# Two-layer diffusion-transformer block: two feed-forward weight chunks loaded into other buffers, and ScalarE's order at the turn from mixer to feed-forward

## The chip, the cores and the metric

The kernel runs on one core of one Trainium2 chip. Its time is the device time of one execution in microseconds (us). TensorE multiplies matrices, VectorE and ScalarE work element by element, GpSimd takes a few side jobs, and SyncE issues all DMA transfers. Engines run side by side, each in its own fixed order, and meet only at semaphores.

## What is computed

Two layers over 512 tokens of width 1024 with a context of 256 tokens. Cut to what matters here, one layer is

```python
x = x + g1x * mixer_output(attn_x, rest_x, *out_w)                      # ends in @ w_o
x = x + g2x * conv_ffn(rmsnorm(x, norm2_g[i]) * (1 + sc2x) + sh2x, *ffn_w)

def conv_ffn(h, w_up, w_conv, w_down):
    g, u = jnp.split(h @ w_up, 2, axis=-1)
    return (jax.nn.silu(dwconv3(g, w_conv)) * u) @ w_down
```

The first layer (layer 0) does the same for the context; the second (layer 1) has the 512 tokens alone. Everything is float32. The change touches the place where the mixer's output projection ends and the feed-forward part begins, once in each layer.

## The kernel before

**Numbers in two halves.** Each float32 operand of a matrix product is split in a rounded high half and the rest, the low half, and each product is three matmuls: high by high, high by low, low by high.

**Weights.** The weights come as chunks of 128x1024 (512 KB), numbered in the order of use, 89 to a layer. Of a layer, chunks 15 to 22 are w_o (`C_WO = 15`) and 23 onward the feed-forward part (`C_FF = 23`). SyncE loads chunk c into `w_raw[c % 2]` (`load`, L408); it waits first until the low half of chunk c - 2 has been made, since that is the last read of this buffer. ScalarE copies it to `w_hi[c % 4]` (`split_hi`, the ACTIVATE at L1021), VectorE subtracts into `w_lo[c % 4]` (`split_lo`, the TENSOR_TENSOR at L1340), and counts it in `chunk_lo`, on which TensorE and `load` wait.

**Activations.** The residual X lies with channels on the partitions, in 8 tiles. The output projection goes in 16 jobs `wo[0]` to `wo[15]`: `wo[8 * i + 4 * s + j]` makes channel tile 4i + j for token part s. In layer 0 the parts are the 512 tokens and the 256 of the context; in layer 1 they are two halves of 256. Each job is added to X by VectorE (`update_part`, L1451), squared by ScalarE (`square`, L1028), and the square is added to a sum by VectorE (`add_squares`, L1398).

**Norm.** TensorE sums the squares over the partitions (L675), ScalarE takes the root (L1035), VectorE the reciprocal (L1418). Then each piece of the normed activation H is made in three steps: `scaled` on VectorE (tmp, L1429), `high` on ScalarE (H_hi, L1047), `low` on VectorE (H_lo, L1438). In layer 0 the first channel tile is made in two pieces of 256 tokens, the other seven in one of 512, then eight of the context; in layer 1 there are eight pieces of 256 for each half.

**The turn.** While TensorE computes the last four jobs `wo[12 + j]`, the two other engines go through a loop over j = 0 to 3. All order is written by hand. VectorE (L1768 to L1774):

```python
update_part(1, 1, j)
scaled(nn, j)
if j:
    low(nn, j - 1)
add_squares(nn, 12 + j, *seg[1][1:])
split_lo(c0 + C_FF + j)
```

ScalarE (L1294 to L1300) splits chunk 23 + j first, once job `wo[12 + j]` is through (this frees the chunk's place in `w_hi`), then squares job 12 + j, then makes the high half of piece j. At j = 0 the root of the first part stands between them. After the loop VectorE alternates `scaled` and `low` for the other pieces. TensorE begins the feed-forward part in `up_first` (L944): at step 0 it multiplies channel tile 0 with chunks 23, 24 and 25, at step 1 tile 1, at step 2 tile 2 and, for the first time, chunk 26. It waits for each chunk's `chunk_lo` and for each piece of H_lo. After eight channel tiles of the first part come the same for the second part.

**Buffers.** `ada_raw[0]` and `ada_raw[1]` (128x1024 each) hold columns of the modulation weights, which are worked off in layer 0. In layer 1 the same place in memory holds `qrs` until the last attention score.

Of the kernel before, what the change touches and what calls it, by code (L numbers as in the profile page):

```python
# [20 lines left out]
F32 = mybir.dt.float32  # L21
F32R = mybir.dt.float32r
ALU = mybir.AluOpType
ACT = mybir.ActivationFunctionType
# [26 lines left out]
C_LAT, C_A2, C_HD, C_WO, C_FF = 0, 4, 12, 15, 23  # L51
NCH = C_FF + 6 * FP
SPARE = 4
UNITS = 2 * HEADS
# [74 lines left out]
JOB = job_plan()  # L129
# [23 lines left out]
def build(nc, dram):  # L153
# [38 lines left out]
    w_raw = [sb(f"w_raw{s}", [P, CH]) for s in range(2)]  # L192
    w_hi = [sb(f"w_hi{s}", [P, CH], F32R) for s in range(4)]
    w_lo = [sb(f"w_lo{s}", [P, CH], F32R) for s in range(4)]
# [15 lines left out]
    ada_raw = [ph(f"ada_raw{s}", [P, D]) for s in range(2)]  # L210
# [53 lines left out]
    def sem(name):  # L264
        return ctx.enter_context(nc.semaphore(name))

    def sems(name, n=DEPTH):
        return [sem(f"{name}{i}") for i in range(n)]

    full, free = sems("psum_full", 4), sems("psum_free", 4)  # L270
    chunk_in = sems("chunk_in", 2)
    chunk_hi, chunk_lo, lat_used = sem("chunk_hi"), sem("chunk_lo"), sem("lat_used")
# [22 lines left out]
    def segs(L):  # L295

        return ALL if L == 0 else ALL[:1]

    def nsegs(nn):

        return ALL if nn < 3 else [(0, 0, NX // 2), (0, NX // 2, NX)]

    def width(L):
        return NT if L == 0 else NX
# [71 lines left out]
    def spare_landed(eng):  # L376
        for n in range(2):
            eng.wait_ge(ada_in[n], 16 * ((ADA_N + ADA_SPARE - n + 1) // 2))

    def pieces(nn):  # L380

        first, second = nsegs(nn)
        work = [(kk, first) for kk in range(KD)] + [(kk, second) for kk in range(KD)]
        if nn < 3:
            work[0:1] = [(0, (0, 0, NX // 2)), (0, (0, NX // 2, NX))]
        return work

    def half(nn):

        return len(pieces(nn)) - KD  # L390
# [15 lines left out]
    @block.sync  # L406
    def _(sp):
        def load(c, i=0, per=0):  # L408
            if c >= 2:
                sp.wait_ge(chunk_lo, c - 1 + per * i if per else c - 1)  # L410
            src = dram["w_main"][c + per * i] if per else dram["w_main"][c]
            sp.dma_start(w_raw[c % 2][:], src).then_inc(chunk_in[c % 2], 16)

        def load_ada(n, i=0, per=0, items=0):
            if n >= 2:
# [20 lines left out]
        for kk in (0, KD // 2):  # L436
            ks = slice(kk, kk + KD // 2)
            sp.dma_start(X[:, ks, 0:NX], dram["x"][:, ks]).then_inc(x_in[2 * kk // KD], 16)
            sp.dma_start(X[:, ks, NX:NT], dram["ctx"][:, ks]).then_inc(x_in[2 * kk // KD], 16)
        load_step(0)  # L440
        load(0)
        load_step(1)
        load(1)
        load_step(2)
        load(2)
        load_step(3)
        load(3)
# [6 lines left out]
        for L in range(DEPTH):  # L454
            c0 = NCH * L
# [47 lines left out]
            with sp.Fori(0, (FP - 1) // 2) as i:  # L503
                n = ADA_FF + 2
                for d in range(2):
                    c = c0 + 33 + 6 * d
# [21 lines left out]
    def _(pool):  # L528
# [24 lines left out]
        for L in range(DEPTH):  # L553
# [4 lines left out]
            def step(ins):  # L558
                nonlocal st
                st += 1  # L560
                ins.then_inc(win_st[L], 1)
            pool.wait_ge(h_lo[2 * L], len(pieces(2 * L)))
            for o, n in streams:
                pool.memset(win_p[:, o - PAD:o], 0.0)
# [68 lines left out]
    def _(pe):  # L633
# [37 lines left out]
        def norm_sum(nn, n, out):  # L671

            _, a, b = nsegs(nn)[n]
            pe.wait_ge(ss_done[nn], 2 + (len(DVE_SQUARES) if nn == 0 else (KD + 4 * (nn % 2), 2 * KD)[n]))
            return pe.matmul(out, ones[:], ss[:, a:b], start=nn > 0, stop=True)  # L675

        def norm_sum_job(nn, n):

            job, (_, a, b) = Job(JOB["sum", nn][n]), nsegs(nn)[n]
            job.open(pe)  # L680
            job.filled(norm_sum(nn, n, job.ps(a, b)))

        def part(job, sg, w, wc, x, xk, first, last):

            wsl = slice(wc, wc + P)
            for n, (ww, xx) in enumerate(((w[0], x[0]), (w[0], x[1]), (w[1], x[0]))):
                for _, a, b in sg:
                    ins = pe.matmul(job.ps(a, b), ww[:, wsl], xx[:, xk, a:b], start=first and n == 0,  # L688
                                    stop=last and n == 2)
            return ins  # L690
# [18 lines left out]
        for L in range(DEPTH):  # L709
            sg, c0 = segs(L), NCH * L  # L710
            jobs = [Job(JOB["lat", L] + j) for j in range(3)]
            for n, (kk, (sgn, ta, tb)) in enumerate(pieces(2 * L)):
                if L == 1 and n == SUM_AT:
                    norm_sum_job(2, 1)
                if L == 0 and n in ROWS_AT:
                    ada_rows(ROWS_AT.index(n) + 1)
                if L == 0 and n in TURN_AT:
                    ada_turn(TURN_AT.index(n) + 1)
                if ta == 0 and kk % 2 == 0:
                    pe.wait_ge(chunk_lo, c0 + kk // 2 + 1)  # L720
                pe.wait_ge(h_lo[2 * L], n + 1)
                wo = (kk % 2) * LATW
                for t in range(ta // P, tb // P):
                    if kk == 0 and t % 2 == 0:
                        jobs[t // 2].open(pe)
                    a = 0 if t < qtok(L) else QR
                    o = 512 * (t % 2)
                    last = mm3(jobs[t // 2].ps(o + a, o + LATW), H, (slice(None), kk, slice(P * t, P * (t + 1))),
                               slot(c0 + kk // 2), (slice(None), slice(wo + a, wo + LATW)), kk == 0, kk == KD - 1)
                    if kk == KD - 1 and t % 2 == 1:  # L730
                        jobs[t // 2].filled(last)
                if ta >= NX and kk % 2 == 1 and kk < KD - 1:
                    last.then_inc(lat_used, 1)
# [280 lines left out]
    def _(act):  # L1014
        def split_hi(c, user=None, i=0, per=0):

            if user is not None:
                user.ready(act)
            n = 16 * (c // 2 + 1)
            act.wait_ge(chunk_in[c % 2], n + 8 * per * i if per else n)  # L1020
            act.activation(w_hi[c % 4][:], w_raw[c % 2][:], ACT.Copy).then_inc(chunk_hi, 1)  # L1021

        def square(nn, q, m, a, b, job=None):

            if job is not None:
                job.taken(act)
            act.wait_ge(ss_done[nn], q + 1)
            act.activation(tmp[q % 2][:, a:b], X[:, m, a:b], ACT.Square).then_inc(sq_done[nn], 1)  # L1028
# [4 lines left out]
        def root(nn, src, n):  # L1033
            _, a, b = nsegs(nn)[n]
            return act.activation(ss[:, a:b], src, ACT.Sqrt, bias=vec[:, V_EPS:V_EPS + 1], scale=1.0 / D)  # L1035
# [6 lines left out]
        def high(nn, n):  # L1042
            L, which = nn // 2, nn % 2
            kk, (sg, a, b) = pieces(nn)[n]
            m = 24 * which + kk
            act.wait_ge(t_done[nn], n + 1)
            act.activation(H[0][:, kk, a:b], tmp[kk % 2][:, a:b], ACT.Identity,  # L1047
                           bias=mod[L][:, sg, m:m + 1]).then_inc(h_hi[nn], 1)
# [21 lines left out]
        for n in range(2):  # L1070
            root_job(0, n)
        split_hi(0)
        rows_out(0)
        for L in range(DEPTH):
            c0, w = NCH * L, width(L)
# [208 lines left out]
            nn, wo = 2 * L + 1, JOB["wo", L]  # L1284
# [7 lines left out]
                square(nn, 8 + j, 4 + j, xa, xb, Job(wo[8 + j]))  # L1292
            root_table()
            for j in range(4):  # L1294
                split_hi(c0 + C_FF + j, Job(wo[12 + j]))
                if j == 0:
                    act.wait_ge(sum_done[nn], 1)
                    root(nn, Job(wo[13]).ps(NX, NX + xb), 0).then_inc(root_done[nn], 1)
                square(nn, 12 + j, 4 + j, ya, yb, Job(wo[12 + j]))
                high(nn, j)  # L1300
            for n in range(4, len(pieces(nn))):
                high(nn, n)
                if n == 6:
                    act.wait_ge(sum_done[nn], 2)
                    root(nn, Job(JOB["u0", L] + 3).ps(NT, NT + NC), 1).then_inc(root_done[nn], 1)
# [17 lines left out]
            with act.Fori(0, (FP - 1) // 2) as i:  # L1323
                for d in range(2):
                    c = c0 + C_FF + 4 + 6 * d
# [10 lines left out]
    def _(dve):  # L1336
        def split_lo(c, i=0, per=0):

            dve.wait_ge(chunk_hi, c + 1 + per * i if per else c + 1)
            dve.tensor_tensor(w_lo[c % 4][:], w_raw[c % 2][:], w_hi[c % 4][:].bitcast(F32),  # L1340
                              ALU.subtract).then_inc(chunk_lo, 1)

        def ada_column(n, L, col, ns, i=0, per=0, items=0):
# [117 lines left out]
        for L in range(DEPTH):  # L1461
            c0, w, sg = NCH * L, width(L), segs(L)
# [14 lines left out]
            else:  # L1477
# [17 lines left out]
                for n in range(3, len(pieces(2)) + 1):  # L1495
                    if n < len(pieces(2)):
                        scaled(2, n)
                    low(2, n - 1)
                    if n < 7:
                        for m in range(2 * (n - 3), 2 * (n - 2)):  # L1500
                            add_squares(2, KD + m, NX, NT)
                    if n in (3, 4):
                        split_lo(c0 + n - 1)
            for j in range(3):
                split_lo(c0 + 4 + j)
            for j in range(3):
# [3 lines left out]
                src = job.ps().rearrange("p (t c) -> p t c", t=2)[:, :, a:LATW]  # L1510
# [222 lines left out]
            nn, wo = 2 * L + 1, JOB["wo", L]  # L1733
# [108 lines left out]
            with dve.Fori(0, (FP - 1) // 2) as i:  # L1842
                for d in range(2):
                    c = c0 + C_FF + 4 + 6 * d
# [138 lines left out]
```

## Time and profile before

| what | value |
| --- | --- |
| runs | 1463.34, 1465.48, 1467.68 us; median 1465.48 |
| the profiled execution | 1463.55 us, its span 1461.6 us |
| TensorE (PE) busy | 1415.6 us, 97% of the span |
| VectorE (DVE) busy | 1010.4 us, 69% |
| ScalarE (ACT) busy | 520.9 us, 36% |
| mean granted clock of TensorE | 0.998 |
| DMA | 109 GB/s on average |

Busy shares add up over the whole span, and an engine's share says nothing of a single place. A timeline row gives the start and the duration in us, the engine, the line, the operation and the shapes; in square brackets stands how long the engine stood idle before the row and what it waited for. Durations of neighbours on one engine overlap by about a tenth of a microsecond, so a step is best read from start to start.

### The profile page before, as it was taken

How to read it: one execution, taken by the hardware profiler on the slowest of the kernel's cores; microseconds unless marked ns; L12 is line 12 of the kernel's file. 1: busy time of each engine (PE TensorE's matmuls, PEld its weight loads, DVE VectorE, ACT ScalarE, POOL GpSimd, SP SyncE). 2: the span in 40 equal slices, each digit the busy share in tenths (PEclk: the TensorE clock that was granted, in tenths of full speed). 3: DMA queues.
4: the chain of work that ended last, by engine and by line, in shares of the span. 5: the costliest groups of instructions: out<-in, count | busy, mean ns of one | idle time of the engine just before them, and what ended most of it. 6: DMA issues, size and time to landing. Idle time of an engine off the chain costs nothing.

```text
span 1461.6 us, 20635 instructions
## 1 busy us (share of the span) xinstructions
PE 1415.6 (97%) x7932; PEld 1223.2 (84%) x7932; DVE 1010.4 (69%) x1534; ACT 520.9 (36%) x829; POOL 86.0 (6%) x139
## 2 busy tenths in 40 slices
PE   6999899999999999999999998989999999999999
PEld 3788698879888888888888877868999888888887
DVE  5587988789867666656675688788667555555555
ACT  4352766233222122122121225466445233223222
POOL 0024700000000000000000000350000000000000
PEclk9999999999999999999999999999999999999999
DMA  9742012333643243325333411301023322322324
GB/s 385 283 139 89 1 44 72 129 103 102 200 130 115 91 139 115 108 93 156 116 97 104 140 47 59 115 15 44 15 87 100 102 87 100 100 86 86 111 92 143
DMA packets 42983, 158.62 MB, mean 109 GB/s; under 512 B 5168, under 2 KB 6576, under 8 KB 41776
## 3 DMA queue, kind: packets, MB, share of 16 engines
q1 hardware_dynamic: 42928, 157.87, 32.1%
q8 instruction: 36, 0.59, 0.2%
q14 instruction: 19, 0.16, 0.0%
HBM read 155.76 MB, written 2.10 MB: 108 GB/s over the span
## 4 chain that ended last, share of the span: by engine, by line
PE 83%; DVE 10%; ACT 3%; issue 2%; DMA 2%; SPq 0%; DVEq 0%; ACTq 0%
PE ps L688 67%; PE ps L637 4%; PE ps L638 4%; PE ps L639 4%; DMA ada_step<-in_w_step 1%; DVE tmp L1429 1%; DVE w_lo L1340 1%; DVE H_lo L1438 1%; PE ps L838 1%; DVE ss L1418 1%; PE ps L651 1%; DVE qn L1616 1%; DVE nmax L1643 1%; DVE pt_lo L1444 1%; DVE ss L1398 1%
## 5 line engine op out<-in xcount | busy, mean ns | idle before, releaser
L688 PE MATMUL ps<-H_hi,w_hi 128*128 128x512 f32 (+1 forms) x1280 | 449.4, 351 | 6.8 <-DVE H_lo L1438 3.4
L688 PE MATMUL ps<-H_lo,w_hi 128*128 128x512 f32 (+1 forms) x1280 | 448.2, 350 | 0.0
L688 PE MATMUL ps<-H_hi,w_lo 128*128 128x512 f32 (+1 forms) x1280 | 447.8, 350 | 0.0
L1021 ACT ACTIVATE w_hi<-w_raw 128x1024 fp32r<-128x1024 f32 x180 | 187.5, 1055 | 423.4 <-PE ps L688 368.8
L688 PEld LDWEIGHTS ps<-H_hi,w_hi 128*128 128x128 f32 x1280 | 243.0, 190 | 40.8 <-issue 3.9
L688 PEld LDWEIGHTS ps<-H_hi,w_lo 128*128 128x128 f32 x1280 | 243.0, 190 | 31.5
L688 PEld LDWEIGHTS ps<-H_lo,w_hi 128*128 128x128 f32 x1280 | 243.0, 190 | 30.9
L1451 DVE SCALAR_TENSOR_TENSOR X<-ps,mod,X 128x512 f32<-128x512 f32 (+1 forms) x296 | 180.9, 645 | 108.6 <-PE ps L688 87.5
L1340 DVE TENSOR_TENSOR w_lo<-w_raw,w_hi 128x1024 fp32r<-128x1024 f32 x180 | 221.6, 1241 | 37.4 <-ACT w_hi L1021 36.4
L688 PE MATMUL ps<-inner_hi,w_hi 128*128 128x512 f32 (+1 forms) x528 | 187.6, 355 | 0.3 <-DVE X L1451 0.3
L688 PE MATMUL ps<-inner_lo,w_hi 128*128 128x512 f32 (+1 forms) x528 | 187.2, 355 | 0.0
L688 PE MATMUL ps<-inner_hi,w_lo 128*128 128x512 f32 (+1 forms) x528 | 186.7, 354 | 0.0
L1792 DVE SCALAR_TENSOR_TENSOR tmp<-ps,vec,tmp 128x511 f32<-128x511 f32 (+1 forms) x132 | 87.2, 661 | 133.1 <-ACT tmp L1312 125.4
L1351 DVE SCALAR_TENSOR_TENSOR ada_out<-ada_raw,cb 128x1024 f32<-128x1024 f32 x107 | 130.7, 1222 | 5.1 <-DVE ada_out L1351 0.6
L688 PEld LDWEIGHTS ps<-inner_hi,w_hi 128*128 128x128 f32 x528 | 99.8, 189 | 15.1 <-DVE X L1451 0.7
L688 PEld LDWEIGHTS ps<-inner_lo,w_hi 128*128 128x128 f32 x528 | 99.8, 189 | 14.0 <-issue 0.2
L688 PEld LDWEIGHTS ps<-inner_hi,w_lo 128*128 128x128 f32 x528 | 99.7, 189 | 14.1
L1312 ACT ACTIVATE tmp<-ps,vec 128x768 f32<-128x768 f32 (+1 forms) x44 | 35.0, 795 | 198.9 <-PE ps L688 198.9
L1808 DVE TENSOR_TENSOR ff_v<-tmp,ps 128x768 f32<-128x768 f32 (+1 forms) x44 | 36.1, 820 | 74.7 <-PE ps L688 74.4
L1047 ACT ACTIVATE H_hi<-tmp,mod 128x256 fp32r<-128x256 f32 (+1 forms) x67 | 38.2, 574 | 58.9 <-DVE tmp L1429 58.8
L1315 ACT ACTIVATE tmp<-tmp 128x768 f32<-128x768 f32 (+1 forms) x44 | 32.6, 741 | 71.1 <-DVE tmp L1792 71.1
L1028 ACT ACTIVATE tmp<-X 128x256 f32<-128x256 f32 (+2 forms) x53 | 27.3, 518 | 60.8 <-DVE X L1451 55.9
(192 smaller groups left out, 1845.0 us busy)
## 6 DMA issues: line engine op xcount, KB each, us to landing
w_raw<-in_w_main SPq DMA_DIRECT2D x182, 512.0 KB, 3.2
ada_raw<-in_w_ada SPq DMA_DIRECT2D x73, 512.0 KB, 4.2
ada_step<-in_w_step SPq DMA_DIRECT2D x7, 2048.0 KB, 14.7
X<-in_x SPq DMA_DIRECT2D x2, 1024.0 KB, 6.9
cb<-in_cvec SPq DMA_DIRECT2D x2, 1024.0 KB, 7.2
out_x<-X SPq DMA_DIRECT2D x8, 256.0 KB, 4.5
rtab<-in_rope SPq DMA_DIRECT2D x4, 384.0 KB, 7.2
X<-in_ctx SPq DMA_DIRECT2D x2, 512.0 KB, 8.0
```

The source lines that it names most:

```text
L637: pe.matmul(out, wh[wsl], xh[xsl], start=first, stop=False)
L638: pe.matmul(out, wh[wsl], xl[xsl], start=False, stop=False)
L639: return pe.matmul(out, wl[wsl], xh[xsl], start=False, stop=last)
L688: ins = pe.matmul(job.ps(a, b), ww[:, wsl], xx[:, xk, a:b], start=first and n == 0, stop=last and n == 2)
L1021: act.activation(w_hi[c % 4][:], w_raw[c % 2][:], ACT.Copy).then_inc(chunk_hi, 1)
L1047: act.activation(H[0][:, kk, a:b], tmp[kk % 2][:, a:b], ACT.Identity, bias=mod[L][:, sg, m:m + 1]).then_inc(h_hi[nn], 1)
L1312: act.activation(tmp[par][:, 0:w], g.ps(0, w), ACT.Copy, scale=tap).then_inc(ff_mid[L], 1)
L1340: dve.tensor_tensor(w_lo[c % 4][:], w_raw[c % 2][:], w_hi[c % 4][:].bitcast(F32), ALU.subtract).then_inc(chunk_lo, 1)
L1351: dve.scalar_tensor_tensor(ada_out[:], ada_raw[n % 2][:], 1.0, cb[n >= ADA_A2][:, s], ALU.mult, ALU.mult, accum_out=mod[L][:, s, bass.ds(c ...
L1451: last = dve.scalar_tensor_tensor(xo, job.ps(a - o, b - o), mod[L][:, s, bass.ds(gate + m, 1)], xo, ALU.mult, ALU.add)
L1792: ins = dve.scalar_tensor_tensor(y, g.ps(a + s0, b - 1 + s0), vec[:, bass.ds(L * V_LAYER + V_FC + FT * tap + t, 1)], y, ALU.mult, ALU.add)
L1808: u.last_read(dve.tensor_tensor(ff_v[:, 0:w], tmp[par][:, 0:w], u.ps(0, w), ALU.mult))
```

## The change

For layer 1, chunks 25 and 26 (in the code `NCH + C_FF + 2` and `NCH + C_FF + 3`) are loaded into `ada_raw[0]` and `ada_raw[1]`. Their loads no longer wait for `chunk_lo` but for the earlier loads that count in the same semaphore, and for the last attention score. For both layers, ScalarE's loop at the turn is reordered: with j = 0 as before, and for j = 1 to 3 the square first, then the high half of H, then the weight split, which no longer has a wait for the job of its own. VectorE's and TensorE's orders are left as they are.

```diff
+    SPARE_RAW = (NCH + C_FF + 2, NCH + C_FF + 3)
+
+    def raw_of(c):
+
+        return ada_raw[SPARE_RAW.index(c)] if c in SPARE_RAW else w_raw[c % 2]
...
         def load(c, i=0, per=0):
-            if c >= 2:
+            if c in SPARE_RAW:
+                sp.wait_ge(chunk_in[c % 2], 16 * (c // 2))
+                Job(JOB[("s", UNITS - 1, 1), 1]).ready(sp)
+            elif c >= 2:
                 sp.wait_ge(chunk_lo, c - 1 + per * i if per else c - 1)
             src = dram["w_main"][c + per * i] if per else dram["w_main"][c]
-            sp.dma_start(w_raw[c % 2][:], src).then_inc(chunk_in[c % 2], 16)
+            sp.dma_start(raw_of(c)[:], src).then_inc(chunk_in[c % 2], 16)
...
-            act.activation(w_hi[c % 4][:], w_raw[c % 2][:], ACT.Copy).then_inc(chunk_hi, 1)
+            act.activation(w_hi[c % 4][:], raw_of(c)[:], ACT.Copy).then_inc(chunk_hi, 1)
...
             for j in range(4):
-                split_hi(c0 + C_FF + j, Job(wo[12 + j]))
                 if j == 0:
+                    split_hi(c0 + C_FF + j, Job(wo[12 + j]))
                     act.wait_ge(sum_done[nn], 1)
                     root(nn, Job(wo[13]).ps(NX, NX + xb), 0).then_inc(root_done[nn], 1)
                 square(nn, 12 + j, 4 + j, ya, yb, Job(wo[12 + j]))
                 high(nn, j)
+                if j:
+                    split_hi(c0 + C_FF + j)
...
-            dve.tensor_tensor(w_lo[c % 4][:], w_raw[c % 2][:], w_hi[c % 4][:].bitcast(F32),
+            dve.tensor_tensor(w_lo[c % 4][:], raw_of(c)[:], w_hi[c % 4][:].bitcast(F32),
                               ALU.subtract).then_inc(chunk_lo, 1)
```

## Rows read from the trace of the kernel before

**Rows 1.** The chain that ended last, in order of time: start us, us, what
```profile
328.99 526.96 PE ps L688 x3042
...
1089.20 3.22 DMA w_raw<-in_w_main
...
1111.44 346.57 PE ps L688 x1563
```

**Rows 2.** Timeline of TensorE where it stood idle at the two turns
```profile
319.54 0.47 PE L688 MATMUL ps<-H_hi,w_hi 128*128 128x512 f32 x1 [2.07 <-DVE H_lo L1438]
...
325.54 0.50 PE L688 MATMUL ps<-H_hi,w_hi 128*128 128x512 f32 x1 [0.59 <-DVE H_lo L1438]
...
1095.52 0.38 PE L688 MATMUL ps<-H_hi,w_hi 128*128 128x256 f32 x1 [1.87 <-DVE w_lo L1340]
```

**Rows 3.** Timeline of VectorE, layer 1, before, at and behind the turn
```profile
1070.60 1.23 DVE L1340 TENSOR_TENSOR w_lo<-w_raw,w_hi 128x1024 fp32r<-128x1024 f32 x1 [0.60 <-ACT w_hi L1021]
...
1089.09 0.48 DVE L1451 SCALAR_TENSOR_TENSOR X<-ps,mod,X 128x256 f32<-128x256 f32 x1
...
1090.61 1.22 DVE L1340 TENSOR_TENSOR w_lo<-w_raw,w_hi 128x1024 fp32r<-128x1024 f32 x1
1091.74 0.48 DVE L1451 SCALAR_TENSOR_TENSOR X<-ps,mod,X 128x256 f32<-128x256 f32 x1
...
1093.90 0.43 DVE L1398 TENSOR_TENSOR ss<-ss,tmp 128x256 f32<-128x256 f32 x1 [0.89 <-ACT tmp L1028]
...
1098.04 0.48 DVE L1429 SCALAR_TENSOR_TENSOR tmp<-X,amul,ss 128x256 f32<-128x256 f32 x1
...
1110.90 0.48 DVE L1438 SCALAR_TENSOR_TENSOR H_lo<-tmp,mod,H_hi 128x256 fp32r<-128x256 f32 x1 [0.18 <-ACT H_hi L1047]
```

**Rows 4.** Timeline of ScalarE, layer 1, before and at the turn
```profile
1069.51 1.06 ACT L1021 ACTIVATE w_hi<-w_raw 128x1024 fp32r<-128x1024 f32 x1 [1.41 <-PE ps L639]
...
1087.74 0.51 ACT L1047 ACTIVATE H_hi<-tmp,mod 128x256 fp32r<-128x256 f32 x1 [2.10 <-DVE tmp L1429]
1088.15 1.05 ACT L1021 ACTIVATE w_hi<-w_raw 128x1024 fp32r<-128x1024 f32 x1
1089.60 0.42 ACT L1028 ACTIVATE tmp<-X 128x256 f32<-128x256 f32 x1 [0.41 <-DVE X L1451]
1090.00 0.51 ACT L1047 ACTIVATE H_hi<-tmp,mod 128x256 fp32r<-128x256 f32 x1
1092.51 1.06 ACT L1021 ACTIVATE w_hi<-w_raw 128x1024 fp32r<-128x1024 f32 x1 [2.00 <-DMA w_raw<-in_w_main]
```

**Rows 5.** Timeline of VectorE, layer 0, at the turn
```profile
316.72 1.22 DVE L1340 TENSOR_TENSOR w_lo<-w_raw,w_hi 128x1024 fp32r<-128x1024 f32 x1
317.86 0.48 DVE L1451 SCALAR_TENSOR_TENSOR X<-ps,mod,X 128x256 f32<-128x256 f32 x1
318.25 0.74 DVE L1429 SCALAR_TENSOR_TENSOR tmp<-X,amul,ss 128x512 f32<-128x512 f32 x1
...
324.08 0.74 DVE L1429 SCALAR_TENSOR_TENSOR tmp<-X,amul,ss 128x512 f32<-128x512 f32 x1
```

**Rows 6.** Timeline of ScalarE, layer 0, at the turn
```profile
316.11 0.51 ACT L1047 ACTIVATE H_hi<-tmp,mod 128x256 fp32r<-128x256 f32 x1 [1.76 <-DVE tmp L1429]
...
319.03 0.72 ACT L1047 ACTIVATE H_hi<-tmp,mod 128x512 fp32r<-128x512 f32 x1 [0.24 <-DVE tmp L1429]
```

**Rows 7.** Windows: stretch, us, busy us (count) PE, PEld, DVE, ACT, POOL, PEclk, DMA, GB/s
```profile
318.00:319.00 1.00, 0.00 (x0) 0.00 (x0) 1.00 (x3) 0.42 (x1) 0.00 (x0) 1.00 0.08 29
...
1096.00:1098.00 2.00, 2.00 (x14) 2.00 (x13) 2.00 (x4) 0.79 (x3) 0.00 (x0) 0.61 0.73 240
1098.00:1100.00 2.00, 2.00 (x12) 2.00 (x12) 1.93 (x6) 1.02 (x2) 0.00 (x0) 0.54 0.44 131
1100.00:1102.00 2.00, 2.00 (x18) 1.94 (x17) 1.97 (x5) 1.38 (x3) 0.00 (x0) 1.00 0.40 162
```

## The prediction

> **What bounds the kernel now.** I read the chain of waits first. TensorE carries nearly all of it, and between the turns it carries it without a break: 527 us from 329 us on, behind the turn of layer 0, and 347 us from 1111 us to the end, behind that of layer 1 [rows 1]. So nothing later can take up a delay: what a turn loses, the kernel loses. Next I looked for what TensorE waits for at the two turns. In layer 0 it stands idle for 2.07 us before 319.54 and for 0.59 before 325.54, each time for H_lo, a product of VectorE; in layer 1 for 1.87 us before 1095.52, for w_lo of chunk 25, of VectorE too [rows 2]. In layer 1 TensorE then catches up: the last H_lo starts at 1110.90, and the chain leaves VectorE for TensorE at 1111.44, just behind its end [rows 1, 3]. So at both turns VectorE's order sets the end, and I must ask when VectorE gets through its loop. The timelines of VectorE and ScalarE answer it.
>
> In layer 1 the loop's passes j = 1 to 3 go from `update_part` at 1089.09 to the `scaled` behind the loop at 1098.04, 8.95 us [rows 3]. An undisturbed pass takes 2.65 (1089.09 to 1091.74). One wait stands out: 0.89 us before 1093.90, for the square of ScalarE. The square was late since ScalarE had stood 2.00 us before it, for the DMA of chunk 25 [rows 4], whose load was issued at 1089.20 and took 3.22 us [rows 1]. That is what the new buffers address.
>
> **Part 1, the loads in layer 1.** Removed: the wait of chunks 25 and 26 on `chunk_lo`. What their loads wait for instead has long happened: chunk 24 can be loaded once chunk 22 has been split, at 1070.60 plus 1.23 [rows 3], and chunks 25 and 26 follow the landing of 23 and 24. Even one behind the other, three loads of 3.22 us are in by 1082, and ScalarE asks for chunk 25 after 1090. On SyncE's queue the next load, chunk 27, stands behind them, but it waits for chunk 25's low half anyway, and its reader is a job of the feed-forward part behind 1111. Taken alone, with ScalarE's old order, this takes away the 0.89 us, with bounds of 0 and 1.0 (three passes at 2.65 are 7.95). In layer 0 no load changes its buffer.
>
> **Part 2, ScalarE's order, layer 1.** VectorE's order stays: at the end of pass j it wants w_hi of chunk 23 + j. Before, ScalarE had split that chunk ahead of the square; at j = 1 the split started at 1088.15, before `update_part` [rows 4]. Now it is queued behind a square that must wait for this pass's `update_part`, and behind a high half that must wait for this pass's `scaled`. Step by step, from start to start: `update_part` to square 0.51 (1089.09 to 1089.60), square to high half 0.40 (to 1090.00), high half to split 0.41 (1087.74 to 1088.15) [rows 3, 4], split to low half on VectorE 1.09 (1069.51 to 1070.60) [rows 3, 4], low half to the next `update_part` 1.14 (1090.61 to 1091.74, rounded up) [rows 3]. A pass becomes 3.55 us. VectorE's own work ahead of its split ends after 1.52 (1089.09 to 1090.61) [rows 3], ScalarE's result is there only after 2.41, so VectorE stands idle 0.89 us in each pass. Three passes are 10.65 against 8.95, **1.70 us later**, and this already holds the gain of part 1. ScalarE's new order thus gives back the 0.89 and twice as much again.
>
> Who waits for it: everything behind on VectorE, so the other twelve pieces of H, the last of which goes from 1110.90 to 1112.60; and TensorE, whose step 0 gets chunk 25 at 1096.3 and not 1095.5, and chunk 26 at 1099.8. Is TensorE late by itself then? It needs 96 matmuls for the first part, at 18 in 2 us [rows 7], some 10.7 us. With the stop for chunk 26 and the sum it is through at about 1109, and needs less than 3 us more to stand before the last piece. That is before 1112.6, so VectorE's delay is what counts, and TensorE's idle time ahead of chunk 25 is hidden.
>
> **Part 2, layer 0.** The high half at j = 1 starts at 316.11 [rows 6], as before; the split behind it at 316.52, and VectorE's low half at 317.61 in place of 316.72 [rows 5]: 0.89. In passes 2 and 3 the piece is 512 wide: `update_part` to `scaled` 0.39 (317.86 to 318.25) [rows 5], `scaled` to high half 0.78 (318.25 to 319.03) [rows 5, 6], high half to split 0.62 (its 0.72 less the tenth by which neighbours overlap, as 0.51 becomes 0.41 in [rows 4]), then 1.09 and 1.14 as above, in all 4.02. From the low half at 317.61 I get `update_part` at 318.75 and, two passes later, the `scaled` behind the loop at 326.79, against 324.08 [rows 5]: **2.71 us later**. TensorE waited for the H_lo right behind this `scaled` (325.54) [rows 2], and from then on was never short of work, so all of it lands in the time. The load of chunk 26 is issued 0.9 us later too, at about 318.8, and lands at 322; ScalarE asks for it at 324.6, so it costs nothing. Without that cover its 3.2 us would be seen.
>
> **Sum.** 1.70 + 2.71 = 4.4 us, to which I add 0.2 for the clock (below). On the profiled execution (1463.55 us, of which the span is 1461.6) this gives 1468.2. That execution is 1.9 us under the median of the runs, 1465.48; against the median, which I forecast, 1470.1. A measurement of this kernel can tell about 0.3% from no change, that is 4.4 us: the forecast stands just on this bound.
>
> **The clock.** In layer 1 the granted clock was 0.61 and 0.54 from 1096 to 1100, the lower level (1.2 GHz) for most of it, after TensorE had stood idle; 26 matmuls went through where 36 fit at the full level, a loss of 10 by 0.11, 1.1 us [rows 7]. In layer 0, after 2.07 us of idleness, the clock stayed at 1.00, 2.4 GHz [rows 2, 7]. After the change TensorE's idle time in layer 0 is 2.9 us in one piece (to 320.3) and three more of 1.0 to 1.6, so a slow stretch can come there. Bounds: 0, and one or two stretches in the open, 1.1 to 2.2. I take 0.2, near the row with no fall, because a slow stretch before 328.2 lies beside waits for VectorE, and only its tail is seen. The Trainium skill (TensorE: Matmul & The Clock Gate, "What's actually happening") says that the low clock is the default and that activity is what lifts it. By that rule the change works against itself at both turns, as it stretches idleness; the row of layer 1 agrees, that of layer 0 shows that idleness of this size doesn't always cost.
>
> **The rivals.**
> Forecast (chance 0.70): both turns lose, 3.9 to 5.6 us, 1469.4 to 1471.1. For it: VectorE is named by both of TensorE's waits, and the passes follow from rows.
> Rival A, not slower (0.07): ScalarE is ahead after all. Its place is the split in each pass; it decides if square, high half and split together are through within VectorE's 1.52 us. Then layer 1 gains up to 1.0, layer 0 nothing: 1464.5. Against it: the square can't start before 0.51 and the split alone takes 1.09, which is 1.60 without any high half.
> Rival B (0.13): only one turn is paid. TensorE has other work at the other turn (the sum over partitions, parts on hand), or the stretch behind is less dense than the chain has it: +1.7 or +2.7, 1467.2 to 1468.2. Against it: 527 us of chain with no other engine in it [rows 1].
> Rival C (0.10): the clock falls in the open twice, by the page's rule above worked out in this kernel's rows: 4.4 + 2.2, 1472.1. For it, the longer idleness; against it, 1.00 at 318 us [rows 7].
> The change does what it says, as the orders show in the code; that the new buffers are busy at 1072 us would be a wait on the last attention score, over before the output projection begins.
>
> **How the numbers follow.** The likeliest is 1470.1. The runs before span 4.3 us, so I add 2 us of scatter on either side of the cases: 1466.5 takes in most of rival B, 1473.5 rival C. Slower by over 0.3% (above 1469.9): 0.6 of the forecast's 0.70 and all of C, 0.42 + 0.10 = 0.52. Within: the rest of the forecast, B and nearly all of A, 0.46. Faster by over 0.3%: 0.02.
>
> **What would show it.** In layer 1, ScalarE's splits of chunks 25 and 26 no longer wait for a DMA, and VectorE waits for `w_hi` three times, 0.9 us each; the `scaled` behind the loop is 1.7 us further from pass 1's `update_part`, and the last H_lo ends at 1113.1 if the span up to there is unchanged but for layer 0's part. In layer 0, VectorE waits for `w_hi` 0.9, then about 1.1 and 0.7 us, and TensorE's wait ahead of step 2 grows from 0.59. The forecast is wrong if VectorE shows no wait for `w_hi` at the turns, if TensorE is still behind VectorE when the last piece of H is ready, or if the clock falls at other places than now.

## The result, and the profile after

The changed kernel takes 1469.4 us (median of 9 runs, 1467.9 to 1471.21), the kernel before 1465.48; the ratio is 1.0024, 95% interval [1.0016, 1.0032], or 3.5 us more (the two medians lie 3.9 us apart). Run again beside a later series it gave 1.0030 [1.0018, 1.0041]. It is slower, as both intervals lie wholly above 1, and in the first comparison by just less than the 0.3% that I had set as the bound of what can be told.

Both turns went as the working said. In all that follows, a turn is the stretch from the first `update_part` of the last four jobs to the start of TensorE's unbroken stretch. Its ends in the kernel before are these two rows of VectorE's timeline and [rows 1] (328.99 and 1111.44):

```profile
308.02 0.48 DVE L1451 SCALAR_TENSOR_TENSOR X<-ps,mod,X 128x256 f32<-128x256 f32 x1 [0.73 <-PE ps L639]
...
1083.91 0.48 DVE L1451 SCALAR_TENSOR_TENSOR X<-ps,mod,X 128x256 f32<-128x256 f32 x1 [1.49 <-PE ps L639]
```

In the changed kernel (lines behind the first edit have moved by 9 to 11), first the same rows of VectorE, then those of the chain in order of time:

```profile
308.80 0.48 DVE L1462 SCALAR_TENSOR_TENSOR X<-ps,mod,X 128x256 f32<-128x256 f32 x1 [0.73 <-PE ps L648]
...
1088.21 0.48 DVE L1462 SCALAR_TENSOR_TENSOR X<-ps,mod,X 128x256 f32<-128x256 f32 x1 [1.49 <-PE ps L648]
```
```profile
23.21 3.61 PE ps L660 x16
...
332.47 526.96 PE ps L697 x3042
...
1117.41 346.58 PE ps L697 x1563
```

Layer 0's turn grows from 20.97 to 23.67 us, layer 1's from 27.53 to 29.20: 2.70 and 1.67, in all 4.37. The unbroken stretches behind them are as long as before, to 0.01 us [rows 1], so nothing took the delay up. The two profiled executions lie 6.0 us apart in span, and the other 1.6 lie outside the turns. 0.78 us are there before the first turn begins: the first 16 matmuls on the modulation's weights took 3.61 us in the row above and 1.92 in the kernel before; from 23 to 26 us the granted clock was 0.54 here and 1.00 there. The other 0.8 us lie between the first unbroken stretch and the second turn, at the layer boundary. Neither place was changed. This is why I read the experiments by their turns first and by their times second.

Why the turns grew, in VectorE's timeline of layer 1, to be read against [rows 3]:

```profile
1093.40 0.48 DVE L1462 SCALAR_TENSOR_TENSOR X<-ps,mod,X 128x256 f32<-128x256 f32 x1
...
1095.80 1.23 DVE L1351 TENSOR_TENSOR w_lo<-w_raw,w_hi 128x1024 fp32r<-128x1024 f32 x1 [0.80 <-ACT w_hi L1030]
1096.94 0.48 DVE L1462 SCALAR_TENSOR_TENSOR X<-ps,mod,X 128x256 f32<-128x256 f32 x1
...
1099.33 1.23 DVE L1351 TENSOR_TENSOR w_lo<-ada_raw,w_hi 128x1024 fp32r<-128x1024 f32 x1 [0.79 <-ACT w_hi L1030]
...
1102.87 1.23 DVE L1351 TENSOR_TENSOR w_lo<-ada_raw,w_hi 128x1024 fp32r<-128x1024 f32 x1 [0.79 <-ACT w_hi L1030]
1104.01 0.48 DVE L1440 SCALAR_TENSOR_TENSOR tmp<-X,amul,ss 128x256 f32<-128x256 f32 x1
...
1116.87 0.48 DVE L1449 SCALAR_TENSOR_TENSOR H_lo<-tmp,mod,H_hi 128x256 fp32r<-128x256 f32 x1 [0.18 <-ACT H_hi L1056]
```

The wait for the square in [rows 3], and the wait of ScalarE for the DMA that had caused it [rows 4] are gone. In their place stand three waits of 0.8 us for the high half of the weight, one in each pass. A pass takes 3.54 us (1093.40 to 1096.94), the three together 10.61 (to 1104.01), where they took 8.95. The reason is on ScalarE, against [rows 4]:

```profile
1093.91 0.42 ACT L1037 ACTIVATE tmp<-X 128x256 f32<-128x256 f32 x1 [1.35 <-DVE X L1462]
1094.31 0.51 ACT L1056 ACTIVATE H_hi<-tmp,mod 128x256 fp32r<-128x256 f32 x1
1094.72 1.04 ACT L1030 ACTIVATE w_hi<-w_raw 128x1024 fp32r<-128x1024 f32 x1
1097.45 0.42 ACT L1037 ACTIVATE tmp<-X 128x256 f32<-128x256 f32 x1 [1.69 <-DVE X L1462]
1097.84 0.51 ACT L1056 ACTIVATE H_hi<-tmp,mod 128x256 fp32r<-128x256 f32 x1
1098.26 1.04 ACT L1030 ACTIVATE w_hi<-ada_raw 128x1024 fp32r<-128x1024 f32 x1
```

ScalarE is idle for 1.35 and 1.69 us ahead of each square, waiting for VectorE, and VectorE then waits for the split that stands behind the square. Two engines take turns where they had run side by side. In layer 0 VectorE's waits are 0.79, 1.00 and 0.74 us:

```profile
318.38 1.23 DVE L1351 TENSOR_TENSOR w_lo<-w_raw,w_hi 128x1024 fp32r<-128x1024 f32 x1 [0.79 <-ACT w_hi L1030]
...
322.39 1.22 DVE L1351 TENSOR_TENSOR w_lo<-w_raw,w_hi 128x1024 fp32r<-128x1024 f32 x1 [1.00 <-ACT w_hi L1030]
...
326.41 1.23 DVE L1351 TENSOR_TENSOR w_lo<-w_raw,w_hi 128x1024 fp32r<-128x1024 f32 x1 [0.74 <-ACT w_hi L1030]
```

TensorE's idle rows, against [rows 2]:

```profile
321.20 0.77 PE L697 MATMUL ps<-H_hi,w_hi 128*128 128x512 f32 x1 [2.96 <-DVE H_lo L1449]
329.02 0.50 PE L697 MATMUL ps<-H_hi,w_hi 128*128 128x512 f32 x1 [0.53 <-DVE H_lo L1449]
```
```profile
1100.61 0.39 PE L697 MATMUL ps<-H_hi,w_hi 128*128 128x256 f32 x1 [2.66 <-DVE w_lo L1351]
1115.83 0.39 PE L697 MATMUL ps<-H_hi,w_hi 128*128 128x256 f32 x1 [0.30 <-DVE H_lo L1449]
```

At 1115.8 TensorE stands waiting piece by piece: it has caught up with VectorE, so its 2.66 us of idleness ahead of chunk 25 are hidden in layer 1, and VectorE's delay is what counts. In layer 0 the waits between the two rows shown depend on the clock: this execution has 0.53 us ahead of step 2, the repeat of the same kernel 1.26.

### The profile page after: what moved, and what is told of

It is laid out like the page before. It is cut to its first block, busy times and chain, and to the rows that moved or that the text cites. A ratio compares the mean times of both kernels' runs of the same rounds, so it can differ in the third digit from the quotient of the medians.

```text
span 1467.6 us, 20631 instructions
## 1 busy us (share of the span) xinstructions
PE 1421.2 (97%) x7932; PEld 1227.3 (84%) x7932; DVE 1010.8 (69%) x1534; ACT 521.2 (36%) x829; POOL 83.5 (6%) x139
## 4 chain that ended last, share of the span: by engine, by line
PE 83%; DVE 10%; ACT 3%; issue 2%; DMA 1%; SPq 0%; DVEq 0%; ACTq 0%
PE ps L697 67%; PE ps L646 4%; PE ps L648 4%; PE ps L647 4%; DMA ada_step<-in_w_step 1%; DVE w_lo L1351 1%; DVE tmp L1440 1%; PE ps L660 1%; ACT w_hi L1030 1%; PE ps L847 1%; DVE ss L1429 1%; DVE H_lo L1449 1%; DVE nmax L1654 1%; DVE qn L1627 1%; DVE pt_lo L1455 1%
```

## The experiments

All of them in one table: the turns from each profile, their sum less the kernel before's 48.50 us, and the measured ratio to the kernel before. Each ratio belongs to its own series of runs, beside the kernel before in the same series.

| kernel | turn 0 | turn 1 | sum less before | ratio, 95% interval |
| --- | --- | --- | --- | --- |
| before | 20.97 | 27.53 | | |
| changed | 23.67 | 29.20 | +4.37 | 1.0024 [1.0016, 1.0032] |
| changed, again | 23.66 | 29.20 | +4.36 | 1.0030 [1.0018, 1.0041] |
| order only | 23.67 | 29.21 | +4.38 | 1.0036 [1.0023, 1.005] |
| order only, again | 23.68 | 29.21 | +4.39 | 1.0026 [1.0015, 1.0037] |
| order in layer 0 only | 23.67 | 27.60 | +2.77 | 1.0016 [1.0007, 1.0025] |
| order in pass 1 only | 22.07 | 28.32 | +1.89 | 1.0012 [1.0003, 1.0021] |
| buffers only | 21.12 | 26.56 | -0.82 | 0.9994 [0.9985, 1.0003] |
| low halves a pass later | 20.87 | 26.57 | -1.06 | 0.9991 [0.9982, 1.0] |
| early first low half | 20.46 | 27.55 | -0.49 | 1.0005 [0.9996, 1.0014] |
| ... with the buffers | 20.53 | 26.60 | -1.37 | 1.0001 [0.9991, 1.001] |
| ... and piece 3 first | 19.52 | 26.60 | -2.38 | 0.9986 [0.9977, 0.9995] |
| ... and split 24 ahead | 19.54 | 26.19 | -2.77 | 0.9976 [0.9967, 0.9985] |

A turn in this table counts in the whole only if the stretch behind it is as long as ever. It is, to 0.02 us (526.96, and 346.56 to 346.58), in every profile but the last one, where the stretch behind the second turn took 348.06 us; more on that below.

**The buffers alone.** The changed kernel with ScalarE's old loop.

```diff
-                if j == 0:
-                    split_hi(c0 + C_FF + j, Job(wo[12 + j]))
+                split_hi(c0 + C_FF + j, Job(wo[12 + j]))
+                if j == 0:
...
-                if j:
-                    split_hi(c0 + C_FF + j)
```

> The change's loads alone; ScalarE keeps the order of the kernel before. Theory A (what costs time is ScalarE's new order, since VectorE then waits 0.8 to 0.9 us in each pass for the weight's high half; the loads by themselves are good): layer 0 as before, in layer 1 passes 1 to 3 take 3 x 2.65 = 7.95 us in place of 8.95, so 1.0 us under the kernel before, 4.4 to 5.4 under the changed one; ScalarE has no wait for w_raw or ada_raw at that turn. Theory B (the loads are what costs: three of them meet at 1072 us and slow the output projection): over the kernel before by 1 us or more, with the matmuls of w_o spread out there. Theory C (the loads buy nothing, since VectorE has another wait next): 0.0.

Layer 1's turn is 0.97 us shorter, its passes 2.65 us each. That is theory A's number, and it falls against C. Against B too: in the output projection, where the three loads would meet, the `update_part` rows are 2.88 us apart (1081.47, 1084.35, 1087.23), as in the kernel before (1078.15, 1081.03, 1083.91). Layer 0's turn is 0.15 longer, though nothing changed there. It has a DMA wait of its own, which the prediction's rows don't show, in the kernel before as well:

```profile
321.20 1.06 ACT L1021 ACTIVATE w_hi<-w_raw 128x1024 fp32r<-128x1024 f32 x1 [1.45 <-DMA w_raw<-in_w_main]
```

There it is just hidden; here the load of chunk 26 landed a little later (a wait of 1.62 us on ScalarE), and VectorE waited 0.19 us for the square behind it. The interval of the whole time still holds 1.0; a gain of 1 us is shown by the trace and only suggested by the measured time.

**ScalarE's order alone.** The kernel before with the changed loop of ScalarE, nothing else.

> ScalarE's new order alone, in both layers; chunks 25 and 26 are loaded into w_raw as before. Theory A: the split of chunk 25 is asked for at about 5 us after the first pass's start and the load, issued at 0.1 us after its start, takes 3.2, so the load is hidden behind ScalarE's own order, and the same for chunk 26: passes of 3.55 us in layer 1, the same time as the changed kernel within 0.3 us, 4.4 us over the kernel before. If the loads' wait were still there (the buffers worth their 0.9 us also under the new order): 5.3 us over the kernel before, with a wait of ScalarE for a DMA at the turn.

Its turns are the changed kernel's to 0.02 us, and ScalarE has no wait for a DMA at layer 1's turn. The first measurement, +0.36%, looked like the other case, so I ran this kernel and the changed one again side by side.

> ScalarE's new order alone, once more. Its turns were those of the changed kernel to 0.01 us, its median over the kernel before was 1 us larger. Theory A (the buffers buy nothing under the new order): the same time as the changed kernel within 0.5 us. If the buffers bought something that the two turns don't show: 1 us more again.

> The changed kernel once more, beside the next one on the same chip. Theory A: turns of 23.67 and 29.2 us, 3.9 to 4.4 us over the kernel before.

1470.01 us with the order alone against 1470.44 for the changed kernel: no difference. Under the new order the buffers buy nothing, since ScalarE comes to chunk 25 late enough for the old load to be there.

**One turn, then one pass.** The new order for layer 0 alone, then for pass 1 alone, on the kernel before.

```diff
+                new = L == 0        # the other kernel: new = j == 1
-                split_hi(c0 + C_FF + j, Job(wo[12 + j]))
+                if j == 0 or not new:
+                    split_hi(c0 + C_FF + j, Job(wo[12 + j]))
...
+                if j and new:
+                    split_hi(c0 + C_FF + j)
```

> The new order of ScalarE in layer 0 alone, everything else as before. Theory A: both turns are paid and add up; here 2.7 us over the kernel before, all between the first update_part of the last four jobs and TensorE's unbroken stretch, none at layer 1's turn. If only one turn were paid: 0 or the whole 4 us.

> The kernel before with ScalarE's new order in pass 1 alone, in both layers: a third of the dose. Theory A: layer 0's turn 0.88 us longer than before. In layer 1 pass 1 takes 3.54 in place of 2.65, pass 2 2.74 in place of 3.64 (the load of chunk 25 is now hidden), pass 3 3.44 in place of 2.66 (the load of chunk 26, issued later, is now seen): 0.77 longer. In all 1.65 us over the kernel before. If the cost of an order grew only with the later passes: nothing in layer 0.

The first: 2.70 us in layer 0 and 0.07 in layer 1. The turns are paid one by one. The second: 1.10 and 0.79 us, for 0.88 and 0.77 expected. In layer 1 the passes were 3.54, 2.76 and, with the late load of chunk 26, 3.43 us, as worked out. In layer 0 the 0.22 us over the 0.88 are in the loop's pass 3: the load of chunk 26 was issued 0.9 us later and was no longer hidden, so that ScalarE's split and the square behind it were late, and VectorE waited 0.24 us for that square. The expectation had seen this in layer 1 and left it out in layer 0.

**The low halves a pass later.** The sharpest test of the cause: VectorE's instructions are the same, ScalarE keeps the new order, only the place at which VectorE comes to the weight moves.

```diff
                 scaled(nn, j)
                 if j:
+                    split_lo(c0 + C_FF + j - 1)
                     low(nn, j - 1)
                 add_squares(nn, 12 + j, *seg[1][1:])
-                split_lo(c0 + C_FF + j)
             for n in range(4, len(pieces(nn)) + 1):
                 if n < len(pieces(nn)):
                     scaled(nn, n)
+                if n == 4:
+                    split_lo(c0 + C_FF + 3)
                 low(nn, n - 1)
```

> The changed kernel, but VectorE makes each weight's low half one pass later (behind the next pass's scaled), so that ScalarE's high half is there when VectorE comes to it. Same instructions, no data path removed. Theory A (the loss is VectorE's idle wait at this place and nothing else): the waits for w_hi go, passes of layer 1 come back to 2.65 us, layer 0 ends its loop as the kernel before; 0.3 to 0.9 us under the kernel before, 4.7 to 5.3 under the changed one. Theory D (it is the later low halves that hurt TensorE, by the waits for chunks 25 and 26): these come no earlier here than in the changed kernel or hardly so, and the loss stays, 3 us or more over the kernel before.

The waits are gone and the whole loss with them: the turns are 5.43 us shorter than the changed kernel's and 1.06 under the kernel before. Of the 1.06, 0.96 are in layer 1, where the buffers alone had gained 0.97. The time is 0.9991, with an interval that reaches 1.0. From VectorE's timeline in layer 1, a pass of 2.66 us again, with no wait ahead of the low half:

```profile
1089.13 0.48 DVE L1462 SCALAR_TENSOR_TENSOR X<-ps,mod,X 128x256 f32<-128x256 f32 x1
1089.92 1.22 DVE L1351 TENSOR_TENSOR w_lo<-w_raw,w_hi 128x1024 fp32r<-128x1024 f32 x1
1091.79 0.48 DVE L1462 SCALAR_TENSOR_TENSOR X<-ps,mod,X 128x256 f32<-128x256 f32 x1
```

The case against theory D needs more than this total, since its premise did not hold: by starts from the first `update_part`, the low halves of chunks 25 and 26 came 0.91 and 2.13 us earlier in layer 0 than in the changed kernel. What speaks against it is the kernel before. These are the first `update_part` and the low halves of chunks 25 and 26 in layer 0, in the kernel before and then in this one:

```profile
308.02 0.48 DVE L1451 SCALAR_TENSOR_TENSOR X<-ps,mod,X 128x256 f32<-128x256 f32 x1 [0.73 <-PE ps L639]
...
319.64 1.22 DVE L1340 TENSOR_TENSOR w_lo<-w_raw,w_hi 128x1024 fp32r<-128x1024 f32 x1
...
322.95 1.22 DVE L1340 TENSOR_TENSOR w_lo<-w_raw,w_hi 128x1024 fp32r<-128x1024 f32 x1
```
```profile
308.88 0.48 DVE L1462 SCALAR_TENSOR_TENSOR X<-ps,mod,X 128x256 f32<-128x256 f32 x1 [0.73 <-PE ps L648]
...
321.56 1.22 DVE L1351 TENSOR_TENSOR w_lo<-w_raw,w_hi 128x1024 fp32r<-128x1024 f32 x1
...
324.36 1.22 DVE L1351 TENSOR_TENSOR w_lo<-w_raw,w_hi 128x1024 fp32r<-128x1024 f32 x1
```

They come 1.06 and 0.55 us later than in the kernel before, and the turn is 0.10 us shorter all the same. In layer 1 it is TensorE's waits for H_lo in the changed kernel, at 1115.8 above, that speak against D.

So ScalarE's order is not bad in itself. It is bad against a VectorE that asks for the weight at the end of the same pass.

**Toward a better kernel.** If VectorE's time at the turn is what counts, its idle time ahead of the reciprocal can be filled, and work that TensorE doesn't wait for yet can stand back.

```diff
                 update_part(1, 1, j)
+                if j == 0:
+                    split_lo(c0 + C_FF)
                 scaled(nn, j)
...
-                split_lo(c0 + C_FF + j)
+                if j == 3 and L == 0:      # third kernel of this group only
+                    low(nn, 3)
+                if j:
+                    split_lo(c0 + C_FF + j)
```

> The kernel before, but VectorE makes the low half of chunk 23 right behind the first update_part, in the time in which it waits for the root, and no longer at the end of pass 0. By theory A (VectorE's time up to the end of its loop is what counts) the reciprocal starts 0.56 us (layer 0) and 0.77 us (layer 1) later and 1.14 us of work is gone behind it. Layer 0's turn 0.55 us shorter, layer 1's about 0.5 (the DMA wait moves from chunk 25 to chunk 26 and keeps 0.9 us), the time 1.0 us under the kernel before. If the buffers' gain could be had by this alone, layer 1's turn would be 1.4 shorter.

> The same, with the two chunks in the buffers of the modulation columns and ScalarE's old order. Theory A: the gains add, layer 0's turn 0.55 us shorter than before, layer 1's 1.4, 1.9 us under the kernel before. If TensorE's own work bounded layer 1's turn by now: 1.0 shorter there, as with the buffers alone.

> The same again, and in layer 0 VectorE makes the low half of piece 3 ahead of chunk 26's, since TensorE stood waiting for that piece. Theory A: TensorE starts its unbroken stretch 1.45 us earlier in layer 0 than in the kernel before (it comes to be bound by its own nine matmuls of step 1), 1.4 in layer 1 as above; 2.8 us under the kernel before, a ratio of 0.998.

In layer 0 the early low half gave 0.51 us (0.55 expected) and the earlier piece 3 another 1.0, to 1.45 in all, as worked out (in the third kernel the loop behind leaves piece 3 out in layer 0). In layer 1 it gave nothing in either kernel, a miss of 0.5 us each. Nor do the times of the first two show a gain: their ratios are 1.0005 and 1.0001, where 1.0 and 1.9 us were expected and the turns gave 0.49 and 1.37. The third is faster than the kernel before by its measured time as well, 0.9986 [0.9977, 0.9995]. ScalarE's and VectorE's timelines of the second kernel show why layer 1 gained nothing:

```profile
1090.31 0.51 ACT L1056 ACTIVATE H_hi<-tmp,mod 128x256 fp32r<-128x256 f32 x1 [2.88 <-DVE tmp L1438]
1090.73 1.04 ACT L1030 ACTIVATE w_hi<-w_raw 128x1024 fp32r<-128x1024 f32 x1
1091.67 0.40 ACT L1037 ACTIVATE tmp<-X 128x256 f32<-128x256 f32 x1
```
```profile
1092.11 0.42 DVE L1407 TENSOR_TENSOR ss<-ss,tmp 128x256 f32<-128x256 f32 x1 [0.31 <-ACT tmp L1037]
```

The reciprocal starts later, so the first high half of H does, and ScalarE's split of chunk 24 is queued behind it and the next square behind that. Pass 1 takes 3.06 us in place of 2.65. It is the same mistake as the change's, made by me: I moved work on one engine and did not ask what the other had queued behind it. The cure is one more move on ScalarE:

```diff
-                split_hi(c0 + C_FF + j, Job(wo[12 + j]))
+                if j != 1:
+                    split_hi(c0 + C_FF + j, Job(wo[12 + j]))
...
                 square(nn, 12 + j, 4 + j, ya, yb, Job(wo[12 + j]))
+                if j == 0:
+                    split_hi(c0 + C_FF + 1, Job(wo[13]))
                 high(nn, j)
```

> The last version with one more move on ScalarE: the high half of chunk 24 ahead of H's first high half. In the two versions before it, VectorE waited 0.31 us in pass 1 of layer 1, since that high half was queued behind a high half of H that the earlier weight split had pushed back by 0.77 us. Theory A: this wait goes, pass 1 of layer 1 takes 2.65 us in place of 3.06, layer 1's turn is 0.4 shorter than there (26.2 us in place of 26.6), layer 0's the same (19.5), 2.8 us under the kernel before. If TensorE's own work bounds layer 1's turn by now: 26.6 again.

The turns came out at 26.19 and 19.54 us, where 26.2 and 19.5 were expected. This kernel takes 1462.54 us, a ratio of 0.9976 [0.9967, 0.9985] to the kernel before: faster than both kernels of this study, by 0.24% and by about 0.5%. That this last move is itself a gain, the turn alone shows. The intervals of this kernel and the one before it overlap, and in the profiled execution the move was more than lost again: the stretch behind the turn took 348.06 us in place of 346.58, as the granted clock fell just behind the turn, where TensorE waits for nothing.

```profile
1109.00:1110.00 1.00, 0.95 (x6) 0.75 (x7) 0.49 (x1) 0.00 (x0) 0.00 (x0) 0.92 0.00 0
1110.00:1111.00 1.00, 1.00 (x6) 1.00 (x6) 0.00 (x0) 0.60 (x2) 0.00 (x0) 0.50 0.00 0
1111.00:1112.00 1.00, 1.00 (x6) 1.00 (x6) 0.85 (x2) 1.00 (x2) 0.00 (x0) 0.50 0.00 0
1112.00:1113.00 1.00, 1.00 (x7) 1.00 (x6) 1.00 (x2) 0.98 (x2) 0.00 (x0) 0.50 0.06 16
1113.00:1114.00 1.00, 1.00 (x9) 1.00 (x9) 0.78 (x1) 0.96 (x2) 0.00 (x0) 0.88 0.00 0
```

The columns are those of [rows 7]; the clock is the number behind the five engines. Since 1107 us TensorE had stood idle three times, for 0.30 us each, waiting for H_lo. How often such a fall comes in this kernel, one profile cannot tell.

## Why the prediction was right

It held, in the main for its reasons. Point by point:

- What bounds: VectorE at both turns, TensorE without slack between them. The stretches of 526.96 and 346.58 us came back unchanged to 0.01 us [rows 1], and rival B (only one turn paid, 0.13) fell with the kernel that has the order in layer 0 alone.
- Part 1: the loads alone take away 0.97 us (0.89, bounds 0 and 1.0). My sum had it inside layer 1's 1.70; the kernel with the order alone shows that under the new order the buffers earn nothing, as the passes of 3.55 us already said.
- Part 2: passes of 3.55 us in layer 1 came at 3.54, 1.70 us later at 1.67; 2.71 us in layer 0 at 2.70. The waits that I had put at 0.9, 1.1 and 0.7 us in layer 0 show as 0.79, 1.00 and 0.74. A wait counts from the end of the row before, and rows of one engine overlap by a tenth, which accounts for the first two. In the third, `add_squares` came 0.1 us sooner than in the kernel before, where it had waited for its square, and VectorE's wait is that much longer.
- Chunk 25 reached TensorE at 1100.61; less the 4.31 us by which pass 1 began later (1093.40 for 1089.09) this is 1096.3, the time worked out. The idle time ahead of it was hidden, as TensorE's waits behind 1115.8 show.
- The clock: 0.2 us was too high by that much. The granted clock did fall in layer 0's turn, in the profile of the changed kernel though not in that of its repeat, and it cost nothing there (below). Rival C, two falls in the open, did not come about in this change. Its mechanism exists: the last kernel above lost 1.48 us to one such fall, where the prediction had put one at 1.1. Rival A, ScalarE ahead after all, fell with the three waits.
- The signs: two of those named in advance misled. The clock fell at a place where it had not before, which was to speak against the forecast, and the turn was the same without the fall. TensorE's wait ahead of step 2 was to grow from 0.59 us; it was 0.53 with the clock down and 1.26 with it up. The end of the loop on VectorE was the sign that did not depend on the clock.
- The size: 4.4 from the turns and 0.2 for the clock, against 3.5 us in the ratio and 4.4 in the repeat. The intervals of both hold 4.4. I gave 0.52 to slower by over 0.3%; the first ratio lies under that bound, the repeat on it. With a forecast on the bound itself, on which side of it the measurement falls is luck. The lower end of the forecast's case, 1469.4, is where the first measurement came out.

## What to carry to other kernels

When two engines share a loop, write down for each hand-over which instruction of this pass the producer must wait for first: an item that needs nothing of this pass (a weight split) belongs ahead of those that do, as long as its data is there. A DMA wait on the side engine can be replaced by a worse wait when the order is changed along with it; try the two parts of such a change alone. And if an order has made the consumer wait, moving the consumer by one pass can win the whole loss back; here it cost nothing.

## What the runs showed of the hardware

In the changed kernel's layer 0 turn, the windows show the granted clock at the lower level (0.50 is 1.2 GHz) from about 320.2 to 327 us. It fell within the 2.96 us for which TensorE stood idle. In the kernel before, with 2.07 us of idleness, it stayed at 1.00. First two lines of the kernel before (see also [rows 7]), then the changed kernel:

```profile
320.00:321.00 1.00, 1.00 (x7) 0.68 (x5) 1.00 (x2) 0.00 (x0) 0.00 (x0) 1.00 0.52 205
321.00:322.00 1.00, 0.89 (x4) 0.40 (x3) 1.00 (x3) 0.80 (x1) 0.00 (x0) 1.00 0.13 20
```
```profile
318.00:320.00 2.00, 0.25 (x3) 0.04 (x1) 1.62 (x3) 0.35 (x1) 0.00 (x0) 1.00 0.00 0
320.00:322.00 2.00, 0.80 (x2) 0.73 (x3) 1.39 (x4) 1.72 (x3) 0.00 (x0) 0.55 0.67 199
322.00:324.00 2.00, 2.00 (x6) 1.42 (x6) 1.61 (x3) 0.36 (x1) 0.00 (x0) 0.50 0.16 64
324.00:326.00 2.00, 1.99 (x6) 1.08 (x5) 1.67 (x4) 1.71 (x3) 0.00 (x0) 0.50 0.67 221
326.00:328.00 2.00, 2.00 (x8) 1.64 (x7) 1.59 (x2) 0.38 (x1) 0.00 (x0) 0.74 0.10 41
```

In the repeat of the same kernel the clock stayed at 1.00 through this turn, after 2.95 us of idleness, and the turn took 23.66 us in place of 23.67. So a fall of the clock in a stretch in which TensorE waits for another engine was free here: the matmuls only filled what was idle.

The same fall in the open is not. At the start it took one group of 16 matmuls from 1.92 to 3.61 us, in a stretch that no kernel here changed, and it came in some executions and not in others. Behind the second turn of the last kernel it cost 1.48 us. Shifts of that kind are as large as the effects of this study. The scatter of 4 to 6 us between runs of one kernel goes along with the clock: in the largest series, 33 runs of the kernel before, the seven with a mean granted clock of 0.997 or more took 1463.3 to 1465.3 us, the eight at 0.993 or less 1465.5 to 1469.0.
